# Four chunks of hi products, then four chunks of lo products: reordering the matmuls of a float32r decoder trunk

## The chip, the cores and the metric

The kernel runs on one core of one Trainium2 chip. The metric is the device time of one launch in microseconds, lower is better. One launch is one Bass program with explicit semaphores; the host only lays data out.

## The reference

```
for i in range(2):                                   # 256 tokens, D = 2048
    hn = rms_norm(h, norm_mix_g[i])
    mix = conv_recurrent_mixer(hn, ...) if i == 0 else stick_breaking_mixer(hn, w_qkv, w_o)
    h = h + mix
    h = h + squared_relu_mlp(rms_norm(h, norm_mlp_g[i]), w_mlp_up[i], w_mlp_down[i])   # 2048 -> 8192 -> 2048
    gate = sigmoid(rms_norm(h, norm_ple_g[i]) @ w_ple_gate[i])
    h = h + (p[i] @ w_ple_proj[i]) * gate
return rms_norm(h, norm_f_g)
```

Everything is float32. Two feed-forward blocks, two gates and the attention's output projection are the parts that matter here. Nearly all of the work is products of a 2048-row slice of a weight matrix with 256 tokens.

## The kernel before

**Precision.** TensorE takes float32r operands. To keep float32 precision each operand is held as a rounded part (hi) and the rest (lo). A product of a weight tile and an activation tile is then two matmuls: the *hi product*, weight hi against activation hi and lo side by side (512 columns, line 398), and the *lo product*, weight lo against activation hi (256 columns, line 404). The hi product leaves hi times lo in the upper half of its PSUM bank, and that half (`cross`) is added in later.

**Groups and chunks.** A group makes two output tiles of 128 channels for all 256 tokens, from 2048 contraction rows. Its weights come in four chunks of 512 rows (4 tiles `q`, 2 output tiles `o`), so a chunk is 8 hi products and 8 lo products and a group is 32 and 32. A group accumulates into two banks of `ps`; groups alternate between two pairs of banks. Each matmul has its own weight load (LDWEIGHTS).

**How a chunk travels.** SyncE loads 512 KB into one of four `raw` buffers once the lo part of the chunk four before has been made. ScalarE (`split`, line 636) waits for the load and for `chunk_used` of the chunk eight before, and copies it rounded into the hi half of one of eight `spl` buffers (`hi_ready`). VectorE (`split`, line 1037) waits for `hi_ready` and writes raw minus hi into the lo half (`lo_ready`). TensorE's `chunk` waits for `lo_ready` of its chunk, does its 16 matmuls in blocks of two hi and two lo, and the last of them raises `chunk_used`. So while TensorE works on one group, the other two engines refill the buffers it has finished, for the group after the next.

**What ScalarE and VectorE do per group, in order.** Four splits (`period`), each waiting as above. Then `take_cross` (ScalarE, waits for the group's last `chunk_used`) and `take_sum` (VectorE, line 1073). In an up group of the feed-forward there follow relu and scale (VectorE, line 1130), square (ScalarE, line 716), hi copy (ScalarE, line 636) and lo rest (VectorE, line 1066), which raises `up_tiles`. In a down group the sum is added to `h` (line 1117).

**Feed-forward.** It runs in four quarters of 8 up groups and 8 down groups. The hidden activations of one quarter are `hid`, 16 tiles, which is `XB` in layer 0. Chunk `j` of a down group reads the tiles `4j` to `4j+3` of `hid`, so chunk 3 needs the tiles that the quarter's last up group makes: `tiles[3]` waits for `up_tiles` of all eight up groups, and the wait stands in `gemm` directly before chunk 3.

**Who uses what.** `first_pair` does the first two groups of a stage chunk by chunk in turn and is not changed. `gemm` does all others. The groups that the change concerns are 6 + 8 + 3 x 16 = 62 in each feed-forward (`mlp`), 6 in each gate (`after_norm`) and 6 in the attention's output (`square`): 142 groups. The recurrent mixer's and the q/k/v groups stay on `gemm`.

Of the kernel before, what the change touches and what calls it, by code (L numbers as in the profile page):

```python
# [28 lines left out]
P = 128  # L29
# [10 lines left out]
NSPL = 8  # L40
# [49 lines left out]
def trunk(nc, xT, pT, par, w_in, w_rg_a, w_rg_x, w_out, w_qkv, w_o, w_up, w_down, w_proj, w_gate, outT):  # L90
    with ExitStack() as ctx:
        def sb(name, shape, dt=F32):
            return ctx.enter_context(nc.sbuf_tensor(name, shape, dt))

        def sem(name):
            return ctx.enter_context(nc.semaphore(name))
# [3 lines left out]
        spl = sb("spl", [P, NSPL, 4, 2, 256], F32R)  # L100
# [49 lines left out]
        ps = ctx.enter_context(nc.psum_tensor("ps", [P, 4, 512], F32))  # L150
# [5 lines left out]
        hi_ready = sem("hi_ready")  # L156
        lo_ready = sem("lo_ready")
        chunk_used = sem("chunk_used")
# [4 lines left out]
        sum_ready = sem("sum_ready")  # L163
# [66 lines left out]
        def counts(base, turns):  # L230


            return base > 0 or not isinstance(turns, int)
# [149 lines left out]

        @block.tensor
        def _(pe):
            def chunk(b, m, it, x, kt0, first, last, tokens_out=False, releases=1):

                pe.wait_ge(lo_ready, it * 8 + (m + 1))
                w = spl[:, m % NSPL, :, :, :]
                for q in range(4):  # L390
                    kt, start, stop = kt0 + q, first and q == 0, last and q == 3
                    for o in range(2):
                        c = slice(o * P, (o + 1) * P)
                        if tokens_out:

                            pe.matmul(ps[:, b + o, :], x[:, kt, 0, c], w[:, q, :, :], start=start, stop=False)  # L396
                        else:
                            pe.matmul(ps[:, b + o, :], w[:, q, 0, c], x[:, kt, :, :], start=start, stop=False)  # L398
                    for o in range(2):
                        c = slice(o * P, (o + 1) * P)  # L400
                        if tokens_out:
                            mm = pe.matmul(ps[:, b + o, 0:256], x[:, kt, 1, c], w[:, q, 0, :], start=False, stop=stop)  # L402
                        else:
                            mm = pe.matmul(ps[:, b + o, 0:256], w[:, q, 1, c], x[:, kt, 0, :], start=False, stop=stop)  # L404
                mm.then_inc(chunk_used, releases)

            def gemm(g, gi, m, it, x, tiles=None, rows=(0, 4, 8, 12), tokens_out=False, mid=None):

                if counts(g - 1, gi):
                    pe.wait_ge(sum_ready, gi + (g - 1))
                for j, row in enumerate(rows):
                    if mid is not None and j == len(rows) // 2:
                        mid()
                    if tiles is not None:
                        pe.wait_ge(*tiles[j])
                    chunk(2 * (g % 2), m + j, it, x, row, j == 0, j == len(rows) - 1, tokens_out)

            def first_pair(g, m, x, tiles, stat=None, releases=1, mid=None):  # L420


                for j in range(4):
                    if j == 2 and mid is not None:
                        mid()
                    pe.wait_ge(*tiles[j])
                    for s in range(2):
                        if j == 0 and g + s > 1:
                            pe.wait_ge(sum_ready, g + s - 1)
                        if j == 3 and s == 1 and stat is not None:  # L430
                            stat()
                        chunk(2 * s, m + 2 * j + s, 0, x, 4 * j, j == 0, j == 3,
                              releases=releases if j == 3 and s == 1 else 1)

            def stats(n, columns=False):

                pe.wait_ge(sq_folded, 16 * (n + 1))
                if n > 0:
                    pe.wait_ge(rstd_ready, n)
                mm = pe.matmul(Z[:, 0, 0:256], onesD[:, :], nacc[:, :], start=True, stop=True)  # L440
                if columns:
                    for t in range(2):
                        mm = pe.matmul(Z[:, 0, 256 + t:257 + t], nacc[:, t * P:(t + 1) * P], onesD[:, 0:1],
                                       start=False, stop=True, skip_group_check=True)
                mm.then_inc(stat_ready, 1)

            def after_res(f):
                return [(res_tiles, f + 2 * j + 2) for j in range(4)]
# [61 lines left out]
            def mlp(g, m, x, hid, f_in, norm, u):  # L510
                first_pair(g, m, x, after_res(f_in), lambda: stats(norm))
                with pe.Fori(1, 4) as i:
                    for s in range(2):
                        gemm(g + s, i * 2, m + 4 * s, i, x)
                with pe.Fori(0, 4) as i:
                    for s in range(2):
                        gemm(g + 8 + s, i * 2, m + 32 + 4 * s, i, hid,
                             [(up_tiles, u + 2 * j + 2) for j in range(4)])
                with pe.Fori(1, 4) as f:
                    with pe.Fori(0, 4) as i:  # L520
                        for s in range(2):
                            gemm(g + s, f * 16 + i * 2, m + 4 * s, f * 8 + i, x)
                    with pe.Fori(0, 4) as i:
                        for s in range(2):
                            gemm(g + 8 + s, f * 16 + i * 2, m + 32 + 4 * s, f * 8 + i, hid,
                                 [(up_tiles, f * 8 + (u + 2 * j + 2)) for j in range(4)])

            def square(g, m, x, tiles, mid):
                first_pair(g, m, x, tiles, mid=mid)
                with pe.Fori(1, 4) as i:  # L530
                    for s in range(2):
                        gemm(g + s, i * 2, m + 4 * s, i, x, tiles)

            def after_norm(g, m, x, f_in, norm):
                first_pair(g, m, x, after_res(f_in), lambda: stats(norm))
                with pe.Fori(1, 4) as i:
                    for s in range(2):
                        gemm(g + s, i * 2, m + 4 * s, i, x)


            pe.wait_ge(consts_ready, 1)
# [60 lines left out]
            with pe.Fori(0, 2) as i:  # L602
                for s in range(4):
                    gemm(G_OUTA + s, i * 4, C_OUTA + 2 * s, i, XB, [(ya_tiles, 1), (ya_tiles, 2)], (0, 4))
            mlp(G_MLP0, C_MLP0, XA, XB, 8, 1, 0)
            after_norm(G_GATE0, C_GATE0, XA, 16, 2)


# [16 lines left out]
            ple(G_PLE1, C_PLE1, 1, range(8))  # L625
            suffix_sums(7, 0)
            square(G_OUT1, C_OUT1, XA, [(att_tiles, 2 * j + 2) for j in range(4)], lambda: values(7, 0, 1))
            mlp(G_MLP1, C_MLP1, XB, XA, 32, 4, 32)
            after_norm(G_GATE1, C_GATE1, XB, 40, 5)
            stats(6)  # L630

# [961 lines left out]
```

## Time and profile before

| | |
|---|---|
| median of three runs | 2404.21 us (2402.06 to 2404.46) |
| the profiled execution | 2405.38 us, of which the span is 2403.7 us |
| TensorE (PE) busy | 2353.1 us, 98% |
| its weight loads (PEld) busy | 2052.8 us, 85% |
| VectorE (DVE), ScalarE (ACT) busy | 67%, 53% |
| mean granted TensorE clock | 0.992 |
| DMA | 179 GB/s over the span |

The busy time of TensorE is modelled from overlapping matmuls, so 98% does not say that it streams at its peak. The distance between the starts of two matmuls tells what one costs. Columns of the timeline: start in us, length in us from the first start to the last end of the row, engine, line, operation, operands, count.

### The profile page before, as it was taken

What the parts mean: (1) busy time and instruction counts of PE and PEld (TensorE: products, weight loads), DVE (VectorE), ACT (ScalarE), POOL (GpSimd) and SP (SyncE); (2) the same over time, 40 slices, a digit from 0 to 9 for tenths busy, and PEclk for the clock granted to TensorE, in tenths of its full rate; (3) what the DMA queues carried; (4) which work ended last, traced back from release to release, by engine and by line L of the source; (5) the groups of instructions that cost most, each with busy time, mean ns of one, the idle gap of its engine ahead of it and who ended that gap; (6) DMA issues with size and microseconds to landing.
All of it is one profiled execution on the core that took longest, in us unless ns stands there. A gap on an engine that the chain in (4) does not pass through costs nothing.

```text
span 2403.7 us, 39317 instructions
## 1 busy us (share of the span) xinstructions
PE 2353.1 (98%) x13454; PEld 2052.8 (85%) x13454; DVE 1600.6 (67%) x1892; ACT 1277.2 (53%) x1632; POOL 2.1 (0%) x15
## 2 busy tenths in 40 slices
PE   7999999999999999999999999999999999999997
PEld 6878878888888888888888888888888888888886
DVE  7789987655555555667766666766556556556665
ACT  6665565444444545555565666555445445445553
POOL 0000000000000000000000000000000000000000
PEclk9999999999999999999999999999999999999998
DMA  7644456655665666555655554656656566565553
GB/s 232 210 123 135 130 163 193 193 185 182 197 187 181 195 189 185 187 189 166 201 172 177 168 157 142 208 183 189 193 180 198 185 187 192 188 188 187 190 161 105
DMA packets 432146, 431.03 MB, mean 179 GB/s; under 512 B 13136, under 2 KB 430032, under 8 KB 432080
## 3 DMA queue, kind: packets, MB, share of 16 engines
q1 hardware_dynamic: 432080, 430.20, 57.5%
q8 instruction: 36, 0.59, 0.1%
q14 instruction: 30, 0.25, 0.0%
HBM read 428.05 MB, written 2.10 MB: 179 GB/s over the span
## 4 chain that ended last, share of the span: by engine, by line
PE 91%; DVE 4%; ACT 2%; issue 1%; DMA 1%; DVEq 0%; SPq 0%; ACTq 0%
PE ps L398 56%; PE ps L404 28%; PE ps L396 2%; PE O L576 2%; DVE spl L1037 1%; PE ps L402 1%; ACT spl L636 1%; PE ps L461 0%; PE O L505 0%; DVE tv L1073 0%; PE Z L479 0%; DMA raw<-in_w_o 0%; DMA raw<-in_w_in 0%; DVE nacc L1101 0%; DVE tv L1099 0%
## 5 line engine op out<-in xcount | busy, mean ns | idle before, releaser
L1037 DVE TENSOR_TENSOR spl<-raw,spl 128x1024 fp32r<-128x1024 f32 x810 | 979.6, 1223 | 521.1 <-ACT spl L636 482.5
L636 ACT ACTIVATE spl<-raw 128x1024 fp32r<-128x1024 f32 x810 | 842.9, 1055 | 685.6 <-PE ps L404 640.9
L398 PE MATMUL ps<-XA,spl 128*128 128x512 f32 x3072 | 971.1, 398 | 15.9 <-DVE spl L1037 10.9
L398 PE MATMUL ps<-XB,spl 128*128 128x512 f32 x3072 | 967.5, 396 | 0.5 <-DVE pp L1073 0.5
L404 PEld LDWEIGHTS ps<-XA,spl 128*128 128x128 f32 x3072 | 579.2, 189 | 137.2
L404 PEld LDWEIGHTS ps<-XB,spl 128*128 128x128 f32 x3072 | 577.1, 188 | 136.4
L404 PE MATMUL ps<-XA,spl 128*128 128x256 f32 x3072 | 605.2, 278 | 0.0
L404 PE MATMUL ps<-XB,spl 128*128 128x256 f32 x3072 | 603.6, 278 | 0.0
L398 PEld LDWEIGHTS ps<-XA,spl 128*128 128x128 f32 x3072 | 470.4, 189 | 17.6 <-issue 11.5
L398 PEld LDWEIGHTS ps<-XB,spl 128*128 128x128 f32 x3072 | 468.3, 189 | 1.6 <-issue 0.8
L1073 DVE TENSOR_TENSOR tv<-cross,ps 128x512 f32<-128x512 f32 x208 | 141.6, 681 | 39.4 <-ACT cross L636 39.2
L636 ACT ACTIVATE cross<-ps 128x512 f32<-128x512 f32 x224 | 130.3, 582 | 68.8 <-PE ps L404 57.2
L716 ACT ACTIVATE tv<-tv 128x512 f32<-128x512 f32 x64 | 40.4, 631 | 138.5 <-DVE tv L1130 138.5
L1117 DVE TENSOR_TENSOR h<-h,tv 128x512 f32 (+1 forms) x104 | 72.0, 692 | 21.1 <-DVE tv L1073 18.8
L396 PE MATMUL ps<-spl,XB 128*128 128x512 f32 x256 | 80.7, 397 | 0.0
L689 ACT ACTIVATE tv<-h 128x512 f32 (+1 forms) x56 | 35.4, 632 | 59.0 <-DVE h L1117 56.1
L1066 DVE TENSOR_TENSOR XB<-tv,XB 128x512 f32 (+1 forms) x32 | 22.2, 692 | 54.0 <-ACT XB L636 54.0
L402 PEld LDWEIGHTS ps<-spl,XB 128*128 128x128 f32 x256 | 48.1, 188 | 11.4
L1066 DVE TENSOR_TENSOR XA<-tv,XA 128x512 f32 (+1 forms) x32 | 22.2, 692 | 53.4 <-ACT XA L636 53.4
L576 PE MATMUL O<-glu,dg 128*128 (+1 forms) x200 | 47.1, 389 | 3.7 <-ACT dg L892 3.7
L402 PE MATMUL ps<-spl,XB 128*128 128x256 f32 x256 | 50.4, 278 | 0.0
L1367 DVE SCALAR_TENSOR_TENSOR y<-glu,params,y 128x256 f32<-128x256 f32 (+1 forms) x116 | 48.7, 478 | 0.8 <-DVE glu L1079 0.5
(145 smaller groups left out, 885.7 us busy)
## 6 DMA issues: line engine op xcount, KB each, us to landing
raw<-in_w_up SPq DMA_DIRECT2D x256, 512.0 KB, 3.9
raw<-in_w_down SPq DMA_DIRECT2D x256, 512.0 KB, 3.5
raw<-in_w_qkv SPq DMA_DIRECT2D x96, 512.0 KB, 4.4
raw<-in_w_in SPq DMA_DIRECT2D x64, 512.0 KB, 4.2
raw<-in_w_gate SPq DMA_DIRECT2D x64, 512.0 KB, 4.3
raw<-in_w_out SPq DMA_DIRECT2D x32, 512.0 KB, 3.4
raw<-in_w_o SPq DMA_DIRECT2D x32, 512.0 KB, 4.6
raw<-in_w_proj SPq DMA_DIRECT2D x8, 512.0 KB, 4.3
```

The source lines that it names most:

```text
L396: pe.matmul(ps[:, b + o, :], x[:, kt, 0, c], w[:, q, :, :], start=start, stop=False)
L398: pe.matmul(ps[:, b + o, :], w[:, q, 0, c], x[:, kt, :, :], start=start, stop=False)
L402: mm = pe.matmul(ps[:, b + o, 0:256], x[:, kt, 1, c], w[:, q, 0, :], start=False, stop=stop)
L404: mm = pe.matmul(ps[:, b + o, 0:256], w[:, q, 1, c], x[:, kt, 0, :], start=False, stop=stop)
L576: pe.matmul(O[:, 0, 0:256], dg[:, k % NDG, :], glu[:, bass.ds(pair * 2 + 1, 1), k:k + T], start=(k == 0), stop=(k == CA_PE - 1), skip_grou ...
L636: return act.activation(out, in_, ACT.Copy, scale=scale)
L716: act.activation(tv[:, :, :], tv[:, :, :], ACT.Square).then_inc(up_sq, 1)
L1037: dve.tensor_tensor(s[:, :, 1, :], raw[:, m % NRAW, :, :], s[:, :, 0, :].bitcast(F32), ALU.subtract).then_inc(lo_ready, 1)
L1066: return dve.tensor_tensor(X[:, bass.ds(t0, n), 1, :], v, X[:, bass.ds(t0, n), 0, :].bitcast(F32), ALU.subtract)
L1073: dve.tensor_tensor(tv[:, :, :] if out is None else out, cross[:, :, :], ps[:, b:b + 2, 0:256], ALU.add).then_inc(sum_ready, 1)
L1117: dve.tensor_tensor(ht, ht, tv[:, :, :], ALU.add).then_inc(res_ready, 1)
L1367: r = dve.scalar_tensor_tensor(out=o, in0=x, scalar=w, in1=o, op0=ALU.mult, op1=ALU.add)
```

## The change

In `whole`, TensorE does the 32 hi products of a group's four chunks first and then its 32 lo products. The hi products of a chunk wait for `hi_ready` of the chunk instead of `lo_ready`; the lo products wait for `lo_ready`. The buffer of a chunk is released (`chunk_used`) after the chunk's lo products. The waits for `tiles[j]` stand before the hi products of chunk `j`. The two helper functions hold the matmuls as they were.

```
+            def whole(g, gi, m, it, x, tiles=None):
+                b = 2 * (g % 2)
+                if counts(g - 1, gi):
+                    pe.wait_ge(sum_ready, gi + (g - 1))
+                for j in range(4):
+                    if tiles is not None:
+                        pe.wait_ge(*tiles[j])
+                    pe.wait_ge(hi_ready, it * 8 + (m + j + 1))
+                    for q in range(4):
+                        for o in range(2):
+                            hi_product(b, m + j, q, o, x, 4 * j + q, j == 0 and q == 0, False)
+                for j in range(4):
+                    pe.wait_ge(lo_ready, it * 8 + (m + j + 1))
+                    for q in range(4):
+                        for o in range(2):
+                            mm = lo_product(b, m + j, q, o, x, 4 * j + q, j == 3 and q == 3, False)
+                    mm.then_inc(chunk_used, 1)
...
-                        gemm(g + s, i * 2, m + 4 * s, i, x)
+                        whole(g + s, i * 2, m + 4 * s, i, x)
...
-                        gemm(g + 8 + s, i * 2, m + 32 + 4 * s, i, hid,
+                        whole(g + 8 + s, i * 2, m + 32 + 4 * s, i, hid,
                              [(up_tiles, u + 2 * j + 2) for j in range(4)])
```

The other calls of `gemm` in `mlp`, `square` and `after_norm` are replaced in the same way. The programs of SyncE, ScalarE and VectorE are not edited.

TensorE in the first down group of a feed-forward quarter, before: the third and the fourth chunk (`REGISTER_ALU` prepares and carries the wait for the hidden tiles of a chunk).

```order
L388 REGISTER_ALU [waits up_tiles]
L398 MATMUL ps<-XB,spl 128x512 [waits lo_ready]
L398 MATMUL ps<-XB,spl 128x512
L404 MATMUL ps<-XB,spl 128x256 x2
L398 MATMUL ps<-XB,spl 128x512 x2
L404 MATMUL ps<-XB,spl 128x256 x2
L398 MATMUL ps<-XB,spl 128x512 x2
L404 MATMUL ps<-XB,spl 128x256 x2
L398 MATMUL ps<-XB,spl 128x512 x2
L404 MATMUL ps<-XB,spl 128x256 x2
L388 REGISTER_ALU [waits up_tiles]
L398 MATMUL ps<-XB,spl 128x512 [waits lo_ready]
```

The same group in the changed kernel, from the wait of the third chunk on. Line 392 is the hi product there and line 398 the lo product.

```order
L432 REGISTER_ALU [waits up_tiles]
L392 MATMUL ps<-XB,spl 128x512 [waits hi_ready]
L392 MATMUL ps<-XB,spl 128x512 x7
L432 REGISTER_ALU [waits up_tiles]
L392 MATMUL ps<-XB,spl 128x512 [waits hi_ready]
L392 MATMUL ps<-XB,spl 128x512 x7
L398 MATMUL ps<-XB,spl 128x256 [waits lo_ready]
L398 MATMUL ps<-XB,spl 128x256 x7
L398 MATMUL ps<-XB,spl 128x256 [waits lo_ready]
L398 MATMUL ps<-XB,spl 128x256 x7
```

Three chunks of 16 matmuls stood ahead of the last `up_tiles` wait; now three chunks of 8 hi products stand there, and all lo products, with the releases of the buffers, come after it.

## Rows read from the trace of the kernel before

**Rows 1.** The page: span, busy time by engine, TensorE's granted clock in 40 slices.
```profile
span 2403.7 us, 39317 instructions
...
PE 2353.1 (98%) x13454; PEld 2052.8 (85%) x13454; DVE 1600.6 (67%) x1892; ACT 1277.2 (53%) x1632; POOL 2.1 (0%) x15
...
PEclk9999999999999999999999999999999999999998
```

**Rows 2.** All waits of PE in the span: total us, times, longest us.
```profile
PE ps L398 <- DVE spl L1037: 10.9, 1, 10.9
PE Z L440 <- DVE nacc L1101: 10.0, 2, 6.0
PE ps L398 <- DVE tv L1073: 4.5, 3, 2.4
```

**Rows 3.** Busy time by stage, a long piece of each feed-forward (start:end us, span, engines).
```profile
430.00:1110.00 680.00, 680.00 (x3905) 593.19 (x3904) 408.56 (x428) 327.96 (x385) 0.00 (x0) 1.00 0.60 188
1530.00:2240.00 710.00, 710.00 (x4077) 619.38 (x4077) 427.05 (x446) 345.14 (x407) 0.00 (x0) 1.00 0.61 189
```

**Rows 4.** Timeline of PE inside the feed-forward: blocks of two hi, two lo products.
```profile
1000.20 0.63 PE L398 MATMUL ps<-XB,spl 128*128 128x512 f32 x2
1000.67 0.39 PE L404 MATMUL ps<-XB,spl 128*128 128x256 f32 x2
1000.90 0.62 PE L398 MATMUL ps<-XB,spl 128*128 128x512 f32 x2
...
1011.35 0.63 PE L398 MATMUL ps<-XB,spl 128*128 128x512 f32 x2
```

**Rows 5.** Timeline of PE: eighteen 256-column products of the recurrent gates in a row.
```profile
113.41 0.88 PE L556 MATMUL Z<-XB,wrg 128*128 128x256 f32 x6
114.13 1.60 PE L556 MATMUL O<-XB,wrg 128*128 128x256 f32 x12
115.57 0.63 PE L398 MATMUL ps<-XA,spl 128*128 128x512 f32 x2
```

**Rows 6.** Timeline of PE in the per-layer embedding: one hi, one lo in turn.
```profile
316.21 0.40 PE L461 MATMUL ps<-spl 128*128 128x512 f32 x1
316.45 0.28 PE L462 MATMUL ps<-spl 128*128 128x256 f32 x1
316.57 0.40 PE L461 MATMUL ps<-spl 128*128 128x512 f32 x1
...
318.33 0.40 PE L461 MATMUL ps<-spl 128*128 128x512 f32 x1
```

**Rows 7.** Timeline of ACT over the end of a quarter's last up group.
```profile
636.74 1.06 ACT L636 ACTIVATE spl<-raw 128x1024 fp32r<-128x1024 f32 x1 [1.73 <-PE ps L404]
637.71 0.58 ACT L636 ACTIVATE cross<-ps 128x512 f32<-128x512 f32 x1
640.41 0.63 ACT L716 ACTIVATE tv<-tv 128x512 f32<-128x512 f32 x1 [2.13 <-DVE tv L1130]
641.18 0.63 ACT L636 ACTIVATE XB<-tv 128x512 f32 x1
```

**Rows 8.** Timeline of DVE over the same stretch.
```profile
637.83 1.23 DVE L1037 TENSOR_TENSOR spl<-raw,spl 128x1024 fp32r<-128x1024 f32 x1 [1.56 <-ACT spl L636]
638.98 0.68 DVE L1073 TENSOR_TENSOR tv<-cross,ps 128x512 f32<-128x512 f32 x1
639.69 0.69 DVE L1130 SCALAR_TENSOR_TENSOR tv<-tv,rB 128x512 f32<-128x512 f32 x1
642.07 0.69 DVE L1066 TENSOR_TENSOR XB<-tv,XB 128x512 f32 x1 [1.69 <-ACT XB L636]
```

**Rows 9.** Timeline of PE: first block of the next down group, and its chunk 3.
```profile
636.54 0.63 PE L398 MATMUL ps<-XB,spl 128*128 128x512 f32 x2
...
644.90 0.63 PE L398 MATMUL ps<-XB,spl 128*128 128x512 f32 x2
```

**Rows 10.** Timeline of PE: one lo product inside a block, and the next hi.
```profile
1003.57 0.27 PE L404 MATMUL ps<-XB,spl 128*128 128x256 f32 x1
1003.68 0.63 PE L398 MATMUL ps<-XB,spl 128*128 128x512 f32 x2
```

**Rows 11.** The page: DMA issues of the feed-forward weights, KB each, median us to landing.
```profile
raw<-in_w_up SPq DMA_DIRECT2D x256, 512.0 KB, 3.9
```

More of the change, by code:

```diff
@@ L385, in _, with hi_product, lo_product @@
         def _(pe):
+            def hi_product(b, m, q, o, x, kt, start, tokens_out):
+                c, w = slice(o * P, (o + 1) * P), spl[:, m % NSPL, :, :, :]
+                if tokens_out:
+                    pe.matmul(ps[:, b + o, :], x[:, kt, 0, c], w[:, q, :, :], start=start, stop=False)
+                else:
+                    pe.matmul(ps[:, b + o, :], w[:, q, 0, c], x[:, kt, :, :], start=start, stop=False)
+            def lo_product(b, m, q, o, x, kt, stop, tokens_out):
+                c, w = slice(o * P, (o + 1) * P), spl[:, m % NSPL, :, :, :]
+                if tokens_out:
+                    return pe.matmul(ps[:, b + o, 0:256], x[:, kt, 1, c], w[:, q, 0, :], start=False, stop=stop)
+                return pe.matmul(ps[:, b + o, 0:256], w[:, q, 1, c], x[:, kt, 0, :], start=False, stop=stop)
             def chunk(b, m, it, x, kt0, first, last, tokens_out=False, releases=1):
                 pe.wait_ge(lo_ready, it * 8 + (m + 1))
-                w = spl[:, m % NSPL, :, :, :]
                 for q in range(4):
-                    kt, start, stop = kt0 + q, first and q == 0, last and q == 3
                     for o in range(2):
[L393 to L398, printed above, removed]
-                    for o in range(2):
[L400 to L404, printed above, removed]
+                        hi_product(b, m, q, o, x, kt0 + q, first and q == 0, tokens_out)
+                    for o in range(2):
+                        mm = lo_product(b, m, q, o, x, kt0 + q, last and q == 3, tokens_out)
                 mm.then_inc(chunk_used, releases)
@@ L521, in mlp @@
                         for s in range(2):
-                            gemm(g + s, f * 16 + i * 2, m + 4 * s, f * 8 + i, x)
+                            whole(g + s, f * 16 + i * 2, m + 4 * s, f * 8 + i, x)
                     with pe.Fori(0, 4) as i:
                         for s in range(2):
-                            gemm(g + 8 + s, f * 16 + i * 2, m + 32 + 4 * s, f * 8 + i, hid,
+                            whole(g + 8 + s, f * 16 + i * 2, m + 32 + 4 * s, f * 8 + i, hid,
                                  [(up_tiles, f * 8 + (u + 2 * j + 2)) for j in range(4)])
@@ L531, in square @@
                     for s in range(2):
-                        gemm(g + s, i * 2, m + 4 * s, i, x, tiles)
+                        whole(g + s, i * 2, m + 4 * s, i, x, tiles)
             def after_norm(g, m, x, f_in, norm):
@@ L537, in after_norm @@
                     for s in range(2):
-                        gemm(g + s, i * 2, m + 4 * s, i, x)
+                        whole(g + s, i * 2, m + 4 * s, i, x)
             pe.wait_ge(consts_ready, 1)
```

## The prediction

> **What bounds the kernel now.** I read the page first, then TensorE's waits, then its timeline in one steady stretch. The page gives PE 2353.1 of 2403.7 us [rows 1], and the reader is to see there that every other engine has a third of its time or more to spare. In the table of PE's waits the three largest entries are 25.4 us together [rows 2]; the only one for a lo part is a single wait of 10.9 us at the start of the program, so none recurs from group to group. In the long stretches of feed-forward PE is busy without a gap, 680.00 of 680.00 and 710.00 of 710.00 us, at the full clock of 2.4 GHz (granted clock 1.00), while DVE works 60% and ACT 48% of the time [rows 3]. So in the 142 groups of the change the time is the number of matmuls times the distance between their starts. There is no wait to remove: the lo part of a chunk is made a whole group ahead of its use. The looser wait on `hi_ready` is therefore worth nothing, and what decides is whether the new order alters the distance between matmuls, and whether the later releases and the earlier tile wait make someone late.
>
> **Part 1: the order of hi and lo products.** In a steady stretch sixteen blocks of two hi and two lo lie between 1000.20 and 1011.35 [rows 4]: 11.15 us for a group, 0.697 a block. Within a block the two hi take 0.47 (1000.20 to 1000.67) and the two lo 0.23. So a hi costs 0.233 and a lo, in a pair between hi products, 0.115 to 0.116. The change makes no matmul more or less, it makes runs of 32 of a kind. No such run of 512 columns is in the trace, but a run of 256 columns is: eighteen products of the same form (fresh weights, float32r, 256 columns) start from 113.41 to 115.57 [rows 5], 2.16 us, 0.120 each. That is 0.004 more than a lo costs today, and it does not depend on a change of bank, since the first six, into another tensor, take 0.72 too. A second row shows that the order counts. In the per-layer embedding hi and lo alternate singly, and six pairs start from 316.21 to 318.33 [rows 6]: 0.353 a pair, against 0.697/2 = 0.348 in the blocks.
>
> For the hi run I bound the price from both sides. The upper end is what a hi takes today, 0.233. The lower end assumes that the sum is conserved: if a lo really costs 0.120 and the block shifts 0.004 of that onto the hi's, a hi is 0.348 - 0.120 = 0.228. I take 0.233, since the start of the second hi after the first is measured directly under the same conditions that hold throughout a run (a hi streams while the weights of the next hi are loaded), and since 0.233 + 0.120 is exactly the 0.353 of the alternating pairs. A new group is then 32 x 0.233 + 32 x 0.120 = 7.46 + 3.84 = 11.30 us, 0.146 more than 11.15, and 142 groups give **+20.7 us**; at the lower end of the hi price it is 11.14, and the term is zero. Below zero is possible too, if runs stream better than blocks; that is the third rival below.
>
> The Trainium skill has a rule for this distance (TensorE: Matmul & The Clock Gate, Back-to-back issue gap): at the full clock the gap is columns / 2.4 plus about 2.5 ns. By it a hi would be 0.216 and a lo 0.109, the same in any order, a group 10.4 us before and after, and this term zero. The trace does not agree on the size: 0.233 and 0.120 stand in rows 4 and 5.
>
> **Part 2: the releases come later, and in a burst.** A group used to release a buffer every 2.79 us. Now it releases none during 7.46 us of hi products and then four, 0.96 us apart, the last one at its end. The refill is for the group after the next, so ACT's hi copies have a whole group (11.3 us) from the last release to the first hi product that needs them, and the lo copies 7.5 us more. The work is four copies of about 1.0 us and four rests of about 1.15 [rows 7, 8]: done some 3 us after the group's end. The raw loads are issued by the lo rests, so they bunch as well: four of 512 KB in 3.5 us, where one takes 3.9 to land [rows 11]. Four in a row at today's 188 GB/s [rows 3] would need 11.2 us, and they have until the next group's first release, about 8.4 us after the end, for the first and 11.3 for the last. This is covered, and if it were not, a copy that is 2 us late still has 8 us before TensorE asks. I cost it at nothing.
>
> **Part 3: the last tiles of each quarter.** Here a cover goes. Take E as the start of the first down group, 636.54 [rows 9]. Before, ACT's last split starts at E + 0.20 and the cross copy at E + 1.17 [rows 7]; DVE's rest starts at E + 1.29, the sum at E + 2.44, relu at 3.15, and the last lo rest ends at 642.07 + 0.69 = E + 6.22 [rows 8]. TensorE asks for this tile before chunk 3, at 644.90 = E + 8.36 [rows 9], so 2.14 us were to spare. After the change two things move. First, the tile is later: releases are at E - 2.88, - 1.92, - 0.96 and 0. ACT copies from E - 2.68 on, 0.97 apart, and the cross copy starts at E + 1.20, hardly later. DVE starts its four rests at E - 1.59 and they follow each other at 1.15: - 0.44, 0.71, 1.86, and the sum starts at E + 3.01 instead of 2.44. The tile lands at 6.22 + 0.57 = E + 6.79. Second, TensorE asks earlier: after 24 hi products, at E + 24 x 0.233 = E + 5.59. It waits 1.20 us. Behind this wait on TensorE stand the last 8 hi products and all 32 lo products of the group, so nothing is done meanwhile, and no later slack gives it back since TensorE has none. That happens once a quarter, 4 x 2 = 8 times: **+9.6 us**. The bounds are 0.6 us (if DVE is not late) and 1.7 (if the chain loses another half microsecond): 5 to 14 us. I expect the clock to stay at its full level across so short a wait; if it fell, the stretch behind it would run at half of it, and the term would be larger.
>
> Other tile waits: `square` asks for tiles that its `first_pair` already waited for, and gates pass no tiles. The `first_pair` of the next stage takes the residual tile of its last predecessor only after six chunks of 16 matmuls, 6 x 2.79 = 16.7 us on, so a sum that is 0.6 to 1.3 us later is covered there. The waits on `sum_ready` of the bank pair are for a group that ended 11 us before. The final norm has no splits ahead of it.
>
> **Sum.** 20.7 + 9.6 = +30.3 us. The profiled execution's 2405.38 (span 2403.7 and 1.7 around it) would become 2435.7; it lies 1.2 above the median of the runs, so against the median I predict 2404.2 + 30.3 = **2434.5 us**.
>
> **The rivals.**
> (a) *The distance is conserved, and only the stall is left.* A product costs what it costs in any order, the 0.115 of a lo in a block being a part of 0.120 that the hi before it carries. A group then stays at 11.15 us, and the time is 2404.2 + 9.6 = 2413.8. For it speaks that each block has the same sum, 0.697, in a whole stretch of rows; against it the alternating pairs at 0.353. By the rule of the Trainium skill named above this is the case that comes true.
> (b) *More than forecast.* If a hi in a run costs 0.236 and the stalls 1.7 us each, it is 32 x 0.356 = 11.39, +0.24 x 142 = 34, plus 14: 2452.
> (c) *Faster.* Changing from lo to hi and back costs something that a run saves. A lo inside a block starts 0.11 before the next matmul (1003.57 to 1003.68, [rows 10]). If all lo went at 0.11 and all hi at 0.23, a group would be 10.88 us, 0.27 less, and 142 of them -38; with the stall that is 2404.2 - 38.3 + 9.6 = 2375.5. It decides from the point where a group gets 9.6/142 = 0.068 us shorter, 0.001 a product. Against it stand the eighteen products at 0.120.
> (d) *About as before.* The distance is conserved as in (a), and runs save a little of (c), between 0.03 and 0.10 us a group, which pays for the stalls: 2404.2 + 9.6 - 4 to 14, so 2399 to 2409.
>
> **How the numbers follow.** Chances: forecast 0.50, (a) 0.27, (b) 0.05, (c) 0.10, (d) 0.08. The range reaches over (a) with its smaller stalls, 2404.2 + 5 = 2409, down to 2408, and up to the forecast with stalls of 1.7 us and a little on the hi's, 2442. A measurement of this kernel tells 0.2% (4.8 us) from no change. Faster by more than that 0.10, within it 0.09, slower 0.81: even (a) lies 0.4% above.
>
> **What would show it.** In the profile after: starts of hi products in a run at 0.233 (right), 0.228 (rival a) or 0.230 and less (c); of lo products at 0.120 or at 0.11. A new wait of PE's hi product for VectorE's line that writes `XB` or `XA`, 8 times, 1.2 us each. In the groups no wait for `hi_ready` or `lo_ready`. ACT's waits for PE fewer and longer. The prediction is wrong if the 32 hi products of a group do not take 7.4 to 7.5 us, or if PE meets waits elsewhere.

## The result and the profile after

The changed kernel takes 2411.27 us, the median of 8 runs (2410.75 to 2413.94), against 2404.2 for the kernel before (8 runs, 2402.06 to 2405.51). The ratio is 1.0031 with a 95% interval of 1.0021 to 1.0041: 7.1 us slower, where 30.3 were forecast. The direction was right and the time lies in the range, but the likeliest case was not what happened; the time of rival (a), 2413.8 us, comes near it.

The page of the profile after, its span and its busy times, which answer to [rows 1]:

```profile
span 2409.5 us, 39317 instructions
...
PE 2348.0 (97%) x13454; PEld 2066.7 (86%) x13454; DVE 1574.1 (65%) x1892; ACT 1254.0 (52%) x1632; POOL 2.1 (0%) x15
```

PE's waits in the changed kernel (total us, times, longest us). Line 392 is the hi product.

```profile
PE ps L392 <- DVE spl L1060: 10.9, 1, 10.9
PE Z L463 <- DVE nacc L1124: 10.8, 2, 6.0
PE ps L392 <- DVE XA L1089: 5.7, 5, 1.3
PE ps L392 <- DVE XB L1089: 5.1, 4, 1.3
```

The two lower lines are new. They are the waits for the last hidden tiles of a quarter (four in each feed-forward; the fifth for `XA`, 0.4 us, stood in the profile before too). The other waits agree with those of [rows 2] within 0.8 us each, and no group waits for a weight copy.

The timeline of PE over the start of a quarter's down groups shows the wait itself:

```profile
636.50 5.63 PE L392 MATMUL ps<-XB,spl 128*128 128x512 f32 x24
643.38 2.09 PE L392 MATMUL ps<-XB,spl 128*128 128x512 f32 x8 [1.25 <-DVE XB L1089]
```

DVE over the same stretch, which answers to [rows 8]:

```profile
634.91 4.63 DVE L1060 TENSOR_TENSOR spl<-raw,spl 128x1024 fp32r<-128x1024 f32 x4 [2.77 <-ACT spl L659]
639.46 0.68 DVE L1096 TENSOR_TENSOR tv<-cross,ps 128x512 f32<-128x512 f32 x1
640.17 0.69 DVE L1153 SCALAR_TENSOR_TENSOR tv<-tv,rB 128x512 f32<-128x512 f32 x1
642.56 0.69 DVE L1089 TENSOR_TENSOR XB<-tv,XB 128x512 f32 x1 [1.69 <-ACT XB L659]
```

With E = 636.50, the four rests come in one row from the late releases, the sum starts at E + 2.96 (3.01 was worked out) and the tile is ready at 643.25 = E + 6.75 (6.79). TensorE asks after 24 hi products and waits 1.25 us (1.20). This wait is as predicted; what it costs is more, as the account below shows.

The other term is not. The timeline of PE over whole groups:

```profile
1007.93 7.44 PE L392 MATMUL ps<-XB,spl 128*128 128x512 f32 x32
1015.21 4.00 PE L398 MATMUL ps<-XB,spl 128*128 128x256 f32 x32
1019.04 7.44 PE L392 MATMUL ps<-XB,spl 128*128 128x512 f32 x32
```

A group now lies between 1007.93 and 1019.04, 11.11 us, where [rows 4] had 11.15. The 32 lo products take 3.83 us, 0.120 each, as predicted. The 32 hi products take 7.28, which is 0.2275 each and not 0.233. Two more pieces of the same run tell where the old price sits:

```profile
1019.04 1.32 PE L392 MATMUL ps<-XB,spl 128*128 128x512 f32 x5
...
1020.43 5.83 PE L392 MATMUL ps<-XB,spl 128*128 128x512 f32 x25
...
1026.33 3.88 PE L398 MATMUL ps<-XB,spl 128*128 128x256 f32 x31
```

The six hi products that start from 1019.04 on take 1.39 us, 0.232 each; the 26 from 1020.43 to the first lo at 1026.33 take 5.90, 0.2269 each. The starts in the trace, to the nanosecond, are 233, 236, 228, 233 and 230 ns apart behind the lo run and then 227, 227, 226 in turn. So in these runs a hi costs more than 0.227 only in the first five places behind lo products, and blocks of two never leave those places.

The account: 142 groups x -0.034 (11.113 against 11.147 in the traces' starts) = -4.8 us; the eight groups with the wait take 12.65 instead of 11.11, 1.54 each, +12.3 us. The sum is +7.5; measured 7.1. Of the 1.54 us 1.25 are the wait. Another 0.16 are lost because the matmul before the wait runs to its end, 0.39 us from its start, where in the run the next one starts after 0.227: the two starts around the wait at 643.38 are 1.640 us apart. About 0.10 stand in the first distance behind the wait, 0.330 instead of 0.227. The two distances after that are 233 and 231 ns.

The two profiled executions agree with the groups and differ in one thing more. Between their starts and ends the 142 groups are 7.7 us longer together than before, and all the rest is 1.7 us shorter, so the spans lie only 5.9 us apart. These 1.7 us are no gain of the new order: in one stretch of the attention that the change does not touch, the clock fell in the trace of before and not in that of the changed kernel. The rows are busy times by stage as in [rows 3], before and then after; the last three figures are granted clock, DMA share and GB/s:

```profile
1476.40:1479.80 3.40, 1.26 (x8) 0.85 (x6) 1.69 (x3) 2.12 (x3) 0.00 (x0) 1.00 0.00 0
1479.90:1483.20 3.30, 2.79 (x9) 2.41 (x10) 2.10 (x3) 1.33 (x2) 0.00 (x0) 0.50 0.00 0
```

```profile
1476.40:1479.80 3.40, 2.15 (x13) 1.84 (x13) 1.73 (x3) 2.91 (x5) 0.00 (x0) 1.00 0.23 76
1479.90:1483.20 3.30, 0.85 (x6) 0.48 (x4) 1.96 (x3) 1.74 (x3) 0.00 (x0) 1.00 0.00 0
```

Behind 3.4 us with TensorE busy for 1.26, the granted clock is 0.50 (1.2 GHz) for some 3.4 us; at half speed that costs some 1.7 us, an estimate from this row. The unprofiled executions have no trace, so how many of them had such a fall is not known.

### The profile page after: what moved, and what is told of

The parts are those of the page before. It is cut to its first block, busy times and chain, and to the rows that moved or that the text cites. A ratio compares the mean times of both kernels' runs of the same rounds, so it can differ in the third digit from the quotient of the medians.

```text
span 2409.5 us, 39317 instructions
## 1 busy us (share of the span) xinstructions
PE 2348.0 (97%) x13454; PEld 2066.7 (86%) x13454; DVE 1574.1 (65%) x1892; ACT 1254.0 (52%) x1632; POOL 2.1 (0%) x15
## 4 chain that ended last, share of the span: by engine, by line
PE 88%; DVE 6%; ACT 2%; issue 2%; DMA 1%; DVEq 0%; ACTq 0%; SPq 0%
PE ps L392 53%; PE ps L398 28%; DVE spl L1060 2%; PE ps L390 2%; PE O L599 2%; PE ps L397 1%; ACT spl L659 1%; DVE tv L1096 1%; PE O L528 0%; PE Z L502 0%; DMA raw<-in_w_o 0%; PE ps L484 0%; DMA raw<-in_w_in 0%; DVE nacc L1124 0%; DVE tv L1122 0%
## 5 line engine op out<-in xcount | busy, mean ns | idle before, releaser
L1060 DVE TENSOR_TENSOR spl<-raw,spl 128x1024 fp32r<-128x1024 f32 x810 | 953.2, 1221 | 583.0 <-ACT spl L659 577.2
L659 ACT ACTIVATE spl<-raw 128x1024 fp32r<-128x1024 f32 x810 | 814.8, 1055 | 707.0 <-PE ps L398 661.1
L392 PE MATMUL ps<-XA,spl 128*128 128x512 f32 x3072 | 778.6, 393 | 20.8 <-DVE spl L1060 10.9
L392 PE MATMUL ps<-XB,spl 128*128 128x512 f32 x3072 | 791.4, 392 | 5.6 <-DVE XB L1089 5.1
L392 PEld LDWEIGHTS ps<-XA,spl 128*128 128x128 f32 x3072 | 549.0, 189 | 112.2 <-issue 18.1
L392 PEld LDWEIGHTS ps<-XB,spl 128*128 128x128 f32 x3072 | 540.9, 188 | 89.1 <-issue 7.6
L398 PEld LDWEIGHTS ps<-XB,spl 128*128 128x128 f32 x3072 | 438.4, 190 | 45.1
L398 PEld LDWEIGHTS ps<-XA,spl 128*128 128x128 f32 x3072 | 427.7, 191 | 37.7
L398 PE MATMUL ps<-XB,spl 128*128 128x256 f32 x3072 | 447.8, 281 | 0.0
L398 PE MATMUL ps<-XA,spl 128*128 128x256 f32 x3072 | 435.2, 282 | 0.0
```

Source lines behind the costliest of these rows:

```text
L398: return pe.matmul(ps[:, b + o, 0:256], w[:, q, 1, c], x[:, kt, 0, :], start=False, stop=stop)
L659: return act.activation(out, in_, ACT.Copy, scale=scale)
L1060: dve.tensor_tensor(s[:, :, 1, :], raw[:, m % NRAW, :, :], s[:, :, 0, :].bitcast(F32), ALU.subtract).then_inc(lo_ready, 1)
```

## The experiments

All but the two with narrow weight loads were timed in rounds against the kernel before on the same chip. The theory after the result, **A**: the groups gained 0.034 us each, and the eight waits are the whole loss.

**Asking late again.** In the down groups chunk 3 is done on its own after chunks 0 to 2.

```
-                for j in range(4):
+                for part in ((range(4),) if tiles is None else (range(3), range(3, 4))):
...                                     # hi products of the part, then its lo products
```

> The changed kernel, but a down group does hi and lo products of chunks 0 to 2 first and then those of chunk 3, so that TensorE asks for the last hidden tiles 8.3 us into the group, as before. Theory A (the stall at the last tile is the whole loss, and the groups themselves got 0.034 us shorter: 11.113 against 11.147 in the traces): eight stalls of 1.54 us gone, no wait of a hi product for VectorE's XB or XA, 142 x 0.034 = 4.8 us gained: 2399.4 us, ratio 0.998. Rival B (late releases of the weight buffers cost something as well): the down groups still release late, and the time stays above 2404.

It took 2400.84 us, ratio 0.9986 (0.9977 to 0.9995), 10.4 less than the changed kernel. All of PE's waits that are over 1 us in its profile are old ones:

```profile
PE ps L392 <- DVE spl L1061: 10.9, 1, 10.9
PE Z L464 <- DVE nacc L1125: 9.0, 2, 6.0
PE ps L392 <- DVE tv L1097: 4.7, 3, 1.7
PE ps L485 <- DVE pp L1097: 4.4, 3, 2.7
PE ps L485 <- DVE tv L1097: 4.1, 2, 3.9
PE O L600 <- ACT dg L916: 3.7, 1, 3.7
```

So the wait was the whole loss and the order itself gains. Most of the 1.4 us above the expected 2399.4 are in the trace: a down group that is cut takes 11.133 us between starts where an uncut one takes 11.113, and 64 x 0.020 = 1.3 us.

**One kind of group at a time.** First only up groups, gates and attention output in the new order, then only the down groups.

```
-                        whole(g + 8 + s, ...)
+                        gemm(g + 8 + s, ...)
```

> The changed kernel with the down groups back on the order of before; up groups, gates and attention output (78 groups) in the new order. A: no stall, since TensorE asks for the tiles at 8.36 us, and 78 x 0.034 = 2.7 us gained: 2401.5, although the up groups' late releases still delay the tiles by some 0.5 us. B: above 2404.

2401.62 us, ratio 0.9990 (0.9981 to 1.0000): as A says, though the interval just reaches 1.

> The changed kernel with only the 64 down groups in the new order. The tile is then ready at its old time, 6.22 us after the start of the down group, and TensorE asks at 24 x 0.2275 = 5.46. A, with both halves of the stall as predicted (later tile, earlier question): a wait of 0.76 plus the 0.2 that a restart costs, 8 times, 7.7 us, less 64 x 0.034 = 2.2: 2409.7. Rival: if only the later tile made the stall, no wait, 2402.

2410.41 us, ratio 1.0025 (1.0016 to 1.0034), against 2409.7 expected. The wait is there and is shorter, as the timeline of PE shows:

```profile
456.58 5.61 PE L392 MATMUL ps<-XB,spl 128*128 128x512 f32 x24
462.93 2.11 PE L392 MATMUL ps<-XB,spl 128*128 128x512 f32 x8 [0.74 <-DVE XB L1089]
```

The 0.74 us are the wait that the earlier question alone makes (predicted 0.63, which is 1.20 less 0.57); the other 0.5 of the 1.25 come from the later releases in the up groups (predicted 0.57).

**The wait put back.**

```
-                    pe.wait_ge(hi_ready, it * 8 + (m + j + 1))
+                    pe.wait_ge(lo_ready, it * 8 + (m + j + 1))
```

> The changed kernel, but the hi products wait for the lo part of their chunk as before (32 and 32 in the same order). If the looser wait is worth nothing, as predicted, the time is that of the changed kernel, 2411.3, within 0.1%. Rival: if the hi wait hides late copies, the hi products show waits for VectorE's line that writes spl, and the time is above 2414.

2410.55 us against 2411.27, within the scatter of both: the looser wait is worth nothing.

**Is it the number of changes of kind?** If a change from hi to lo and back cost a fixed 0.0022 us, shorter runs inside a chunk would bring most of the gain with no stall.

```
                 for q in range(4):
                     for o in range(2):
                         hi_product(b, m, q, o, x, kt0 + q, ...)
+                for q in range(4):
                     for o in range(2):
                         mm = lo_product(b, m, q, o, x, kt0 + q, ...)
```

> The kernel before, but a chunk does its 8 hi products and then its 8 lo products, in all groups (feed-forward, gates, attention, q/k/v and the mixer); waits and releases stay where they were. Theory A (a change from one kind to the other and back costs about 0.0022 us: 15 of 16 fewer gave 0.034 a group): 12 of 16 changes go, 0.027 a group, in some 200 groups of four chunks and 16 half groups 5.6 us: 2398.6, no stall. Rival C (only the long run of 32 is cheap, its first dozens of products are not): about 2403.

This was a miss: 2409.82 us, ratio 1.0021 (1.0012 to 1.0030), slower than before; its only wait that is longer than before is one of 1.1 us. Its timeline of PE:

```profile
1002.55 2.00 PE L392 MATMUL ps<-XB,spl 128*128 128x512 f32 x8
1004.39 1.12 PE L398 MATMUL ps<-XB,spl 128*128 128x256 f32 x8
1005.35 2.00 PE L392 MATMUL ps<-XB,spl 128*128 128x512 f32 x8
```

A chunk takes 2.80 us (1002.55 to 1005.35), and four blocks of two and two took 2.787. The starts in the trace read 234 236 228 232 231 227 227 226 ns for the hi and 114, then seven times 119 to 120 for the lo. Against 0.2267 and 0.120 each, such a cycle has 0.020 us too much: about 0.027 in the first five hi, less 0.007 in the first lo. A block of two and two has only 0.003 too much, since the lo's after the first two slow hi's come at 113 and 119 or 116 and 112. That is theory **E**: the excess of a change builds up over the first five hi products, and a run pays only if it goes on long past them. Why the first five are slow, no run here shows.

**Alternating singly.**

```
+                        if q > 0 or o > 0:
+                            q1, o1 = (q, 0) if o else (q - 1, 1)
+                            lo_product(b, m, q1, o1, x, kt0 + q1, ...)
```

> The kernel before, but within a chunk hi and lo products alternate singly (hi, lo of the other output tile, hi, ...), in all groups. Theory A: twice the changes of kind, 0.0022 each pair: about 16 x 0.0022 = 0.035 a group more, 7 us: 2411. If the alternating pairs of the per-layer embedding (0.353 a pair against 0.348) show the price of alternating as such: 32 x 0.005 = 0.15 a group, 30 us: 2434. If that price was one of two products in a row into the same bank, which this kernel avoids: 2404 to 2411.

2426.74 us, ratio 1.0091 (1.0076 to 1.0107), between the expectations. Six matmuls of its timeline:

```profile
1002.32 0.40 PE L392 MATMUL ps<-XB,spl 128*128 128x512 f32 x1
...
1003.38 0.40 PE L392 MATMUL ps<-XB,spl 128*128 128x512 f32 x1
```

Three pairs take 1.06 us, 0.353 each. This is the price of [rows 6]. It does not rule out the bank for single alternation: in [rows 6] a hi and the lo behind it write the same bank and the lo and the next hi different ones, here it is the other way round, so each has two neighbours in one bank once a pair. In the blocks and in the runs of four, eight and 32, neighbours never share a bank, so the excess there is not the bank's. A group of the trace takes 11.280 us, 0.033 a chunk more than before and less than 8 x 0.005 = 0.040, since at the seam of two chunks two lo and two hi still stand in a row. The whole is 22.4 us.

**Runs of four,** to test E where it and "fewer changes are cheaper" point in opposite directions.

> The kernel before with each chunk in runs of four hi, four lo, four hi, four lo, in all groups: half as many changes of kind as before. Theory E (a change of kind is paid in the first hi products behind lo products, by the intervals that the traces show there, 233 236 228 233 ns and then 227, and gains 7 ns on the first lo; so a cycle costs 20 ns over 0.2267 and 0.120 each from a run of five on, but only 3.3 ns in a cycle of two and two, which leaves before the later of them come): four hi 0.930, four lo 0.472, 1.402 against 2 x 0.697, +0.017 a chunk, 800 chunks, +13 us: 2417. Rival A (each change costs the same, so fewer are cheaper): 8 fewer a group, -0.018 x 200 = -3.6: 2401.

```
+                for q0 in (0, 2):
+                    for q in (q0, q0 + 1):      # 4 hi products
...
+                    for q in (q0, q0 + 1):      # 4 lo products
```

2418.53 us, ratio 1.0064 (1.0049 to 1.0079): E holds within 1.5 us, with half the changes of kind of before and 14 us more. The timeline:

```profile
1000.68 1.09 PE L392 MATMUL ps<-XB,spl 128*128 128x512 f32 x4
1001.61 0.63 PE L398 MATMUL ps<-XB,spl 128*128 128x256 f32 x4
1002.09 1.09 PE L392 MATMUL ps<-XB,spl 128*128 128x512 f32 x4
1003.01 0.64 PE L398 MATMUL ps<-XB,spl 128*128 128x256 f32 x4
1003.49 1.09 PE L392 MATMUL ps<-XB,spl 128*128 128x512 f32 x4
```

The four hi take 0.93 and the four lo 0.48, 1.40 to 1.41 a cycle against 1.394 for two blocks. The order of the slow places is not always that of E: every second run of four has 235, 233, 236 and 224 ns, with nearly the same sum.

**What is the excess over the columns?** In a long run a hi is 0.0133 over 512 columns at 2.4 GHz (0.2133) and a lo is 0.0133 over 256 (0.1067): the same for both, as if each matmul paid for its weight load. The load was cut to 64, then to 32 columns, the streamed columns left alone. These two kernels leave out most of the sum of half, then of three quarters, of the output channels, and a narrower load also makes the output narrower (64 or 32 rows of the bank), which no run here separates from the load.

```
-                    pe.matmul(ps[:, b + o, :], w[:, q, 0, c], x[:, kt, :, :], start=start, stop=False)
+                    n = P // 2 if half else P
+                    pe.matmul(ps[0:n, b + o, :], w[:, q, 0, o * P:o * P + n], x[:, kt, :, :], start=start, stop=False)
```

> The changed kernel, but in its reordered groups the weight loads have 64 columns instead of 128: all hi products but the first two of a group, all lo products but those of the last two tiles; half of the output channels get only a part of their sum. The columns that stream stay at 512 and 256. A hi costs 0.2275 in a run and a lo 0.1197, both 0.013 to 0.014 over columns / 2.4 GHz. Theory A (the load of the next weights takes the excess, since it is the same for both kinds): the excess halves, hi 0.221, lo 0.113, a group 0.4 us shorter, the span some 2409.5 - 142 x 0.42 = 2350. Rival D (the excess belongs to the matmul or its stream): 0.2275 and 0.1197 stay, and the span is 2409.

> As the run with half weight loads, with 32 columns a load (a quarter of the output channels get the full sum). If the excess of a product over columns / 2.4 GHz follows the load (lo 0.0133 at 128 columns, 0.0067 at 64), lo products come at 0.110. If it stops at some floor, 0.1133 stays. The hi products went from 0.2267 to 0.2300 on average with half loads, which the load does not explain: if that was a beat between stream and load, another average comes out, on either side; if the load matters as for lo, 0.217.

Timelines of PE, 64 columns first, then 32 (a row names the stationary shape of its first matmul, which is still full for the hi runs):

```profile
647.94 7.53 PE L393 MATMUL ps<-XB,spl 128*128 128x512 f32 x32
655.31 3.81 PE L400 MATMUL ps<-XB,spl 128*64 128x256 f32 x32
658.96 7.53 PE L393 MATMUL ps<-XB,spl 128*128 128x512 f32 x32
```

```profile
649.40 7.58 PE L393 MATMUL ps<-XB,spl 128*128 128x512 f32 x32
656.81 3.82 PE L400 MATMUL ps<-XB,spl 128*32 128x256 f32 x32
660.46 7.58 PE L393 MATMUL ps<-XB,spl 128*128 128x512 f32 x32
```

The lo run went from 3.83 to 3.65 us with half loads (most of its starts 0.113 apart, an excess of 0.0067, just half) and stayed at 3.65 with a quarter. The hi run became *longer*: 7.28, 7.37 and 7.41 us. So the expectation that the excess follows the load holds for the lo product at half the load and for nothing else: a floor shows at a quarter, and the hi goes the other way. With narrow loads the hi starts no longer settle at 227 but cycle (224 to 236 ns at 64 columns, 229 to 235 at 32), as if the slow phase behind a change never ended. The single times are 2400.85 and 2406.95 us; the span of the first is 2399.1, 49 us above the 2350 expected. What sets the distance of two hi products is left open.

**Cutting only where the tile is late.** Only the first down group of each quarter does chunk 3 apart, the other 56 do 32 and 32. Run with the version that cuts all, on one chip.

```
+                    whole(g + 8 + s, 0, m + 32 + 4 * s, 0, hid, [...], apart=(s == 0))
+                with pe.Fori(1, 4) as i:
+                    for s in range(2):
+                        whole(g + 8 + s, i * 2, m + 32 + 4 * s, i, hid)
```

> As the run with the late tile wait, but only the first down group of each quarter is cut into chunks 0 to 2 and chunk 3; the other 56 down groups do 32 and 32. No stall. Theory E: 56 fewer pairs of changes, 0.020 each: 1.1 us below the run that cuts all down groups, about 2399.7. Rival: the later release and tiles of the other groups cost something: 2401 or more.

> The run with all down groups cut (chunks 0 to 2, then chunk 3) once more, beside its successor on the same chip: 2400.8 as before.

2398.80 us, ratio 0.9980 (0.9971 to 0.9989), against 2401.09 (0.9989, 0.9980 to 0.9998) for the other. 2.3 us lie between them, 1.1 were expected. The matmul starts of the two traces lie 3.3 us further apart at the end than at the start. Of this the 142 groups make 1.25 us, as E has it, and most of the other 2.0 is a fall of the clock like the one above (granted clock 0.50 from 1478.10 to 1481.30), which only the trace of the version that cuts all has. Its timeline over the start of a quarter's down groups has no wait:

```profile
634.13 5.63 PE L392 MATMUL ps<-XB,spl 128*128 128x512 f32 x24
639.59 3.04 PE L398 MATMUL ps<-XB,spl 128*128 128x256 f32 x24
642.47 2.00 PE L392 MATMUL ps<-XB,spl 128*128 128x512 f32 x8
644.31 1.12 PE L398 MATMUL ps<-XB,spl 128*128 128x256 f32 x8
645.26 7.44 PE L392 MATMUL ps<-XB,spl 128*128 128x512 f32 x32
```

This is the fastest version, 5.6 us below the kernel before.

**Runs of 8 in the remaining groups** on top of the version that cuts all down groups.

> The order that takes what the runs have shown: feed-forward, gates and attention output in runs of 32 (down groups: chunks 0 to 2, then 3), all other groups in runs of 8 by chunk. Theory A: 2400.8 less 60 groups x 0.027 = 1.6: 2399.2. Rival C: 2400.8.

2402.40 us, ratio 0.9991 (0.9982 to 1.0001). Its expectation is older than the result of the runs of eight, and it repeats their miss: 1.3 to 1.6 us slower than without, where E gives some 240 chunks x 0.007 = 1.7.

## Why the prediction was right and wrong

**The bound and the waits: right.** PE's matmul starts were the time, and no wait was there to be removed; putting the old wait back changed nothing.

**Part 1, the order: wrong, and this is the step that failed.** The lo run's price was right, 0.120, read from the eighteen products of [rows 5]. The hi price was taken from the wrong end of its two bounds: 0.233 was chosen, "since the start of the second hi after the first is measured directly under the same conditions that hold throughout a run". The conditions are not the same: the first five hi products behind a lo run are slow, and two in a row never get past them. The run's mean is 0.2275, the lower bound was 0.228. The term was +20.7 us and measured -4.8. The prediction had the fact that gives the lower end, that the block's sum is fixed while a lo alone costs more than its share, and set it aside for the agreement of 0.233 + 0.120 with the 0.353 of the alternating pairs. That sum is the price of single alternation, as the alternating run shows (0.353), and says nothing of runs.

**Part 2, releases in a burst: right.** TensorE waits for no weight copy in the groups, though the median landing of an up load rose from 3.9 us to 4.8; the run that asks for the tiles late gained all of the loss back with the releases still late.

**Part 3, the last tiles: the wait right, its price too small.** 1.25 us against 1.20, in 8 places, and both halves measured apart (0.74 and 0.5). The term was 9.6 and measured 12.3, inside its bounds of 5 to 14: the prediction took the wait for the whole cost, and a wait costs 0.3 more here, 0.16 for the matmul before it that nothing overlaps and 0.10 in the first distance behind it. The clock stayed at 1.00 across these waits, as expected.

**The rivals.** (a), the distance conserved and the stall left, at 2413.8 is 2.5 us from the result and was given 0.27; it should have stood above the forecast. That it comes so near is in part luck: it has nothing for the order, where -4.8 us were measured, and 9.6 for the stalls instead of 12.3. Its reason, that a product costs the same in any order, is not what happens: the order does count, from 2398.8 us to 2426.7 for the same matmuls. What the groups did is what (d) describes, between 0.03 and 0.10 us less each (0.034 measured), given 0.08; its time, 2399 to 2409, was missed by the price of the stalls. (c) had the right sign for the order, at an eighth of its size. The Trainium skill's formula for the gap, columns / 2.4 plus about 2.5 ns, stands in its section for an isolated matmul (TensorE: Matmul & The Clock Gate, Back-to-back issue gap). The traces do not agree with it for this stream of matmuls with fresh weights: the excess over columns / 2.4 is 13.3 ns in long runs.

## What to carry to other kernels

The interval between two instructions in a short pattern need not be the price of either in a long run: where a pattern's sum is known and one member's price alone is known, the difference is the better estimate for the other. In this kernel runs of 24 and 32 of a kind paid, pairs came next, and runs of eight, runs of four and single alternation cost more in that order. With 0.020 us of excess in a long cycle and 0.0033 in a block of two and two, runs would pay from about a dozen of each kind on, an estimate from these two numbers. A wait costs more than its length: 1.54 us for 1.25 of waiting here. When work of a later chunk is moved ahead, look for the one wait that was covered by the work that now comes after it, and cut the order at that place only.

## What the runs showed of the hardware

Float32r matmuls with fresh 128-column weights settle at 0.2267 us for 512 columns and 0.120 for 256, at a granted clock of 1.00, the 2.4 GHz level. In long runs the first five products of 512 columns behind 256-column ones come 233, 236, 228, 233 and 230 ns apart, and the first 256-column product behind 512-column ones gives 7 ns back. The mean of a hi and a lo together is 0.3483 in pairs of two, 0.3508 in runs of four, 0.3492 in runs of eight, 0.3473 in runs of 32 and 0.353 singly.

The Trainium skill says that loading the next tile's weights takes no read bandwidth from the running matmul (TensorE: Matmul & The Clock Gate, Step-by-step: what each phase is for). No run here tests the read bandwidth by itself. What the lo runs show is that the width of the load, or of the output with it, does count in the distance: with half the weight columns a 256-column product came 0.113 after the last instead of 0.120. The hi products got slower with narrower loads (7.28, 7.37, 7.41 us for 32), and no run here explains it.
